# A dense expert mixer whose last 32 tokens take fetched rows instead, with the second table stationary and the gates multiplied on Pool

## The reference, cut to what matters

```python
def peer(xn, w_pq, sub_keys, expert_u, expert_v):       # 8 heads, 16 experts each, of 128*128
    ...
    idx = jnp.take_along_axis(cand_i, sel, axis=-1)
    gates = jax.nn.softmax(top_s, axis=-1)
    def block(args):
        x_blk, i_blk, g_blk = args
        pre = jnp.einsum('tkd,td->tk', expert_u[i_blk], x_blk)
        act = jax.nn.gelu(pre, approximate=False) * g_blk
        return jnp.einsum('tk,tkd->td', act, expert_v[i_blk])

h = h + peer(rms_norm(h, norm_ffn), ...)
gate = jax.nn.sigmoid(rms_norm(h, norm_ple) @ w_ple_gate)
h = h + gate * (p @ w_ple_proj)
return rms_norm(h, norm_final)
```

## Time and profile before

| | |
|---|---|
| time, median of 3 runs | 2223.78 us (2223.14 to 2226.92) |
| the profiled execution's own time | 2223.5 us |
| its span, first to last instruction | 2221.6 us |
| granted TensorE clock, mean | 0.985 of full speed |
| busy: PE, DVE, ACT, Pool | 97%, 69%, 48%, 26% of the span |

### The profile page before, as it was taken

One profiled execution on the slowest core, in us unless ns is written; L12 is line 12 of the kernel. 1 busy time (PEld: TensorE's weight loads), 2 busy tenths in 40 slices (PEclk: granted clock), 3 DMA queues, 4 the chain that ended last, 5 costly groups with the idle time before them and its releaser, 6 DMA issues.

```text
span 2221.6 us, 36663 instructions
## 1 busy us (share of the span) xinstructions
PE 2157.7 (97%) x11170; PEld 1847.3 (83%) x11170; DVE 1532.7 (69%) x2283; ACT 1074.0 (48%) x1444; POOL 573.7 (26%) x295
## 2 busy tenths in 40 slices
PE   7999999979999999999999999999999999999997
PEld 7888878978888888888888888888888888887886
DVE  6885777965547888888865555676677666666665
ACT  6543665234445444444444444545555454555454
POOL 0121000000000688888888881000000000000000
PEclk9999997999999999999999999999999999999998
DMA  5754559035544677777776665766666555654563
GB/s 193 257 184 159 189 178 352 1 128 194 182 170 167 183 182 187 187 184 188 183 195 189 189 188 187 241 244 245 243 241 239 195 190 195 234 191 170 195 202 141
DMA packets 157129, 431.01 MB, mean 194 GB/s; under 512 B 49552, under 2 KB 49936, under 8 KB 155408
## 3 DMA queue, kind: packets, MB, share of 16 engines
q1 hardware_dynamic: 118080, 417.59, 54.4%
q0 software_dynamic: 36864, 0.15, 4.0%
q10 hardware_dynamic: 2128, 12.58, 1.5%
HBM read 409.15 MB, written 21.10 MB: 194 GB/s over the span
## 4 chain that ended last, share of the span: by engine, by line
PE 89%; DVE 5%; DVEq 2%; issue 2%; ACT 1%; DMA 1%; ACTq 0%; SPq 0%
PE ps L237 25%; PE ps L1702 21%; PE ps L241 13%; PE ps L1709 10%; PE ps L262 5%; PE ps L256 5%; PE ps L257 5%; DVE lo L220 1%; PE ps L337 1%; ACT hi L214 1%; PE ps L1599 1%; PE ps L1555 1%; PE ps L1607 1%; DMA raw<-in_w_in_cols 0%; DVEq L879 0%
## 5 line engine op out<-in xcount | busy, mean ns | idle before, releaser
L220 DVE TENSOR_TENSOR lo<-raw,hi 128x1024 fp32r<-128x1024 f32 x724 | 892.6, 1237 | 427.0 <-ACT hi L214 402.4
L214 ACT ACTIVATE hi<-raw 128x1024 fp32r<-128x1024 f32 x724 | 762.7, 1055 | 634.0 <-PE ps L237 442.4
L237 PE MATMUL ps<-act_pair,hi 128*128 128x512 f32 x2816 | 707.8, 393 | 3.7 <-ACT hi L214 3.7
L1459 POOL DMA_INDIRECT gate_map<-gate_in_sb x256 | 529.6, 2069 | 439.9 <-DVEq L1299 361.2
L237 PEld LDWEIGHTS ps<-act_pair,hi 128*128 128x128 f32 x2816 | 507.3, 189 | 96.1 <-ACT hi L214 5.1
L241 PEld LDWEIGHTS ps<-act_pair,lo 128*128 128x128 f32 x2816 | 383.3, 190 | 34.0 <-DVE lo L220 7.3
L241 PE MATMUL ps<-act_pair,lo 128*128 128x256 f32 x2816 | 393.6, 283 | 3.9 <-DVE lo L220 3.9
L1702 PE MATMUL ps<-hi,stage_hi 128*128 128x512 f32 x1024 | 274.3, 390 | 3.3 <-DVE stage_lo L1320 3.2
L1709 PE MATMUL ps<-lo,stage_hi 128*128 128x512 f32 x1024 | 274.5, 390 | 0.0
L1702 PE MATMUL ps<-hi,stage_lo 128*128 128x512 f32 x1024 | 274.2, 390 | 0.0
L802 ACT ACTIVATE stage_hi<-arena 128x256 fp32r (+1 forms) x256 | 107.0, 418 | 344.8 <-PE ps L1709 340.1
(11 more groups left out here) (226 smaller groups left out, 1197.5 us busy)
## 6 DMA issues: line engine op xcount, KB each, us to landing
raw<-in_expert_u SPq DMA_DIRECT2D x256, 512.0 KB
raw<-in_expert_v SPq DMA_DIRECT2D x256, 512.0 KB
raw<-in_w_in_cols SPq DMA_DIRECT2D x64, 512.0 KB
raw<-in_w_in_rows SPq DMA_DIRECT2D x48, 512.0 KB
gate_map<-stage_lo SPq DMA_DIRECT2D x1, 16384.0 KB, 47.4
raw<-in_w_out SPq DMA_DIRECT2D x32, 512.0 KB
raw<-in_w_pq SPq DMA_DIRECT2D x32, 512.0 KB
gate_in_sb<-gate_map SPq DMA_DIRECT2D x32, 512.0 KB, 4.1
```

What stands on the lines that cost most here:

```text
L214: act.activation(hi[:, use, :], raw[:, slot, :], ACT.Copy).then_inc(hi_ready, 1)
L220: dve.tensor_tensor(lo[:, use, :], raw[:, slot, :], hi[:, use, :].bitcast(F32), ALU.subtract).then_inc(lo_ready, 1)
L237: mm = pe.matmul(out_ap, hi[:, use, d8 * P:(d8 + 1) * P], act_pair[:, d, :], start=(d == 0), stop=False)
L1459: pool.indirect_dma_start(gate_map, bass.IndirectOffsetOnAxis(ap=place[:, unit, r:r + 1], axis=0), gates_out[:, unit, r:r + 1], None, comp ...
```

## The change

**Tokens.** The two dense stages take the first 224 tokens (`MANY`). PE moves 448 columns where it moved 512 and 224 where it moved 256 in the U stage; `pre`, the activations, the map and its blocks (448 KB) shrink alike. The scatter of every second unit of gates takes 96 of 128 partitions.

**The V stage.** The table's 128x128 blocks are now held and the activations moved: 8 matmuls of 448 columns with `hi` and 8 of 224 with `lo` for each tile. Sums are channels by tokens and fill all eight banks in either half. Before half 1 may use a bank, DVE empties it (`take_half(0)`, 8 reductions, placed behind the first tile of half 1); behind the last tile comes `take_half(1)`, and `expert_rows` turns the sums back into rows with fp32 matmuls. The tiles are loaded straight out of the table as given: partition p of tile c reads 4 KB of row 128p + c, so neighbouring partitions read 1 MB apart, where before a tile was one contiguous 512 KB.

**The last 32 tokens.** Their 128 picks are dealt to four groups of 32 partitions, 32 steps for each. ACT writes picks, gates and scales to HBM and reads them back spread over the partitions (3 and 17 DMAs, in the last 96 tiles of the U stage). In the V stage Pool fetches for each of 64 steps (32 for the first table, 32 for the second) two halves of 128 x 4 KB by indirect DMA (`gather`), with one buffer for each half; a half is fetched when DVE has used the one before it. DVE's `few_half` multiplies and sums 1024 elements of each partition. Its places are fixed: behind tiles 2, 3, 5, 7 ... 125 of half 0 (64 places, 125/64 tiles apart, rounded down) for the first table, and behind tiles 136 to 248 of the 256 (114/64 apart) for the second. A matmul with a selector adds the four groups.

**The gates.** `apply_gates` moves from DVE to Pool (128x896 instead of 128x1024). Pool's order is `apply_gates(0)`, then for n = 0, 1, ... `apply_gates(n + 1)` (while n + 1 < 32) and `gather(n)`. SP loads block j of the map, as before, behind the table's block j-2 and only once `apply_gates(j-2)` is done.

**What follows.** The tiles of `w_ple` and the first transpose leave half 1 and come behind `expert_rows`, ahead of the gate stage; the second transpose now stands ahead of the first gate tile. DVE's order there is `rest_tile` for `w_ple` tile 0, `take_half(1)`, `add_experts(0)`, tile 1, `add_experts(1)`, tile 2, `take_ple(0)`, first `dve_turn`, tile 3, `take_ple(1)`, `dve_scale`, `take_ple(2)`, gate tile 0, `take_ple(3)`, second `dve_turn`.

The diff, cut to its core:

```diff
+FEW = 32
+MANY = SEQ - FEW
...
-T_PLE = T_V + CHUNKS + PLE_CHUNK
-T_GATE = T_V + 2 * CHUNKS + 4
+T_PLE = T_V + 2 * CHUNKS
+T_GATE = T_PLE + 4
...
-                mm = pe.matmul(out_ap, hi[:, use, d8 * P:(d8 + 1) * P], act_pair[:, d, :], start=(d == 0), stop=False)
+                mm = pe.matmul(first_tokens(out_ap), hi[:, use, d8 * P:(d8 + 1) * P], first_tokens(act_pair[:, d, :]),
+                               start=(d == 0), stop=False)
...
-                mm = pe.matmul(out_ap[:, 0:SEQ], lo[:, use, d8 * P:(d8 + 1) * P], act_hi[:, 8 * k + d8, :],
+                mm = pe.matmul(out_ap[:, 0:tokens], lo[:, use, d8 * P:(d8 + 1) * P], act_hi[:, 8 * k + d8, 0:tokens],
...
+            v_tiles = v_table.rearrange("(p c) (h f) -> h c p f", c=CHUNKS, h=2)
...
-                    load_tile(sp, n, slot, expert_v[ds(j * RAW + k, 1)].rearrange("a p f -> (a p) f"))
+                    n, slot, _, _ = tile_at(T_V + CHUNKS * half, j, RAW, k)
+                    load_tile(sp, n, slot, v_tiles[half][ds(j * RAW + k, 1)].rearrange("a p f -> (a p) f"))
...
+            for g in range(FEW_GROUPS):
+                at = slice(g * FEW, (g + 1) * FEW)
+                picks = slice(g * FEW_STEPS, (g + 1) * FEW_STEPS)
+                act.dma_start(few_index[at], few_ids.rearrange("s q h r -> s q (h r)")[:, :, picks]).then_inc(few_read, 16)
+                act.dma_start(few_gate[at], few_gates.rearrange("s h r -> s (h r)")[:, picks]).then_inc(few_read, 16)
+                act.dma_start(few_stat[at], few_scales).then_inc(few_read, 16)
+                act.dma_start(x_few[at], h_spill[MANY:SEQ, :]).then_inc(few_rows_in, 16)
+            act.dma_start(few_rows, norm_ffn.partition_broadcast(P)).then_inc(few_rows_in, 16)
...
-            def apply_gates(j, buf, turn):
-                dve.wait_ge(map_landed[buf], 16 * turn + 16)
-                a = experts[:, ds(G_CHUNKS * j, G_CHUNKS), :]
-                dve.tensor_tensor(a, a, gate_in_sb[:, buf].rearrange("p (c t) -> p c t", c=G_CHUNKS),
-                                  ALU.mult).then_inc(gated, 1)
-
-            apply_gates(0, 0, 0)
...
+            def few_half(n, q):
+                r, c = n % FEW_STEPS, slice(TILE * q, TILE * (q + 1))
+                dve.wait_ge(few_landed[q], 16 * n + 16)
+                if n < FEW_STEPS:
+                    e = dve.tensor_tensor_reduce(few_rows[:, c], few_rows[:, c], x_few[:, c], 1.0, 0.0, ALU.mult, ALU.add,
+                                                 few_part[:, 2 * r + q:2 * r + q + 1])
+                elif r == 0:
+                    e = dve.tensor_scalar(few_sum[:, c], few_rows[:, c], few_act[:, 0:1], None, ALU.mult)
+                else:
+                    e = dve.scalar_tensor_tensor(few_sum[:, c], few_rows[:, c], few_act[:, r:r + 1], few_sum[:, c],
+                                                 ALU.mult, ALU.add)
...
+            FEW_U_FROM, FEW_U_TO, FEW_V_FROM, FEW_V_TO = 2, 127, 136, 250
+            for k, (n, q) in enumerate(halves_u):
+                FEW_AT[FEW_U_FROM + k * (FEW_U_TO - FEW_U_FROM) // len(halves_u)] = lambda n=n, q=q: few_half(n, q)
...
+            for k, (n, q) in enumerate(halves_v):
+                FEW_AT[FEW_V_FROM + k * (FEW_V_TO - FEW_V_FROM) // len(halves_v)] = lambda n=n, q=q: few_half(n, q)
...
                 v = CHUNKS * half + 4 * i + c
                 dve.wait_ge(stage_hi_ready, v + 1)
-                dve.tensor_tensor(stage_lo[:, c % 2:c % 2 + 1, :], experts[:, ds(4 * i + c, 1), :],
-                                  stage_hi[:, c % 2:c % 2 + 1, :].bitcast(F32), ALU.subtract).then_inc(stage_lo_ready, 1)
-                rest_tile(dve, T_V + v + late, c % RAW, c % SPLIT)
-
-            def gated_block(j, buf, turn, first=False):
+                dve.tensor_tensor(stage[:, c % 2:c % 2 + 1, MANY:2 * MANY], experts[:, ds(4 * i + c, 1), :],
+                                  stage[:, c % 2:c % 2 + 1, 0:MANY].bitcast(F32), ALU.subtract).then_inc(stage_lo_ready, 1)
+                rest_tile(dve, T_V + v, c % RAW, c % SPLIT)
...
+            def take_half(half):
+                dve.wait_ge(lo_used, T_V + CHUNKS * (half + 1))
+                for b in range(8):
+                    dve.tensor_reduce(v_cols[half][:, b], ps[:, b, 0:2 * MANY].rearrange("p (h t) -> p t h", h=2), AX_X,
+                                      ALU.add).then_inc(v_taken, 1)
...
+            for i in range(CHUNKS // 4):
                 for c in range(4):
                     value_tile(1, i, c)
+                    if i == 0 and c == 0:
+                        take_half(0)
+                    few_work(1, i, c)
...
+                        n = P if unit % TB == 0 else FEW_FROM
...
+            def apply_gates(j):
+                pool.wait_ge(map_landed[j % 2], 16 * (j // 2) + 16)
+                if j == G_BLOCKS - 1:
+                    pool.wait_ge(expert_bank, CHUNKS + 2)
+                a = experts[:, ds(G_CHUNKS * j, G_CHUNKS), :]
+                pool.tensor_tensor(a, a, gate_in_sb[:, j % 2, 0:G_CHUNKS * MANY].rearrange("p (c t) -> p c t", c=G_CHUNKS),
+                                   ALU.mult).then_inc(gated, 1)
+
+            def gather(n):
+                r, table = n % FEW_STEPS, u_table if n < FEW_STEPS else v_table
+                for q in range(2):
+                    if n >= 1:
+                        pool.wait_ge(few_done, 2 * n + q - 1)
+                    pool.indirect_dma_start(few_rows[:, q * TILE:(q + 1) * TILE], None,
+                                            table.rearrange("e (h f) -> (e h) f", h=2),
+                                            bass.IndirectOffsetOnAxis(ap=few_index[:, q, r:r + 1], axis=0)
+                                            ).then_inc(few_landed[q], 16)
+
+            pool.wait_ge(expert_bank, CHUNKS - 2)
+            apply_gates(0)
+            pool.wait_ge(few_read, 16 * 3 * FEW_GROUPS)
+            pool.wait_ge(x_few_ready, 2)
+            for n in range(2 * FEW_STEPS):
+                if n + 1 < G_BLOCKS:
+                    apply_gates(n + 1)
+                gather(n)
 
...
-                    for k, a in enumerate((stage_hi, stage_lo)):
-                        for tb in range(TB):
-                            for b in range(2):
-                                mm = pe.matmul(ps[:, 4 * half + 2 * tb + b, :], a[:, use, tb * P:(tb + 1) * P],
-                                               hi[:, use, b * 512:(b + 1) * 512], start=(first and c == 0 and k == 0),
-                                               stop=False, skip_group_check=True)
+                    for b in range(8):
+                        if first and c == 0 and half == 1:
+                            pe.wait_ge(v_taken, b + 1)
+                        if first and c == 0 and half == 0 and b >= U_BANK:
+                            pe.wait_ge(pre_ready, CHUNKS - 1 + b - U_BANK)
+                        mm = pe.matmul(ps[:, b, 0:2 * MANY], hi[:, use, b * P:(b + 1) * P], stage[:, use, 0:2 * MANY],
+                                       start=(first and c == 0), stop=False, skip_group_check=True)
                     mm.then_inc(hi_used, 1)
-                    pe.wait_ge(lo_ready, T_V + v + late + 1)
-                    for tb in range(TB):
-                        for b in range(2):
-                            mm = pe.matmul(ps[:, 4 * half + 2 * tb + b, :], stage_hi[:, use, tb * P:(tb + 1) * P],
-                                           lo[:, use, b * 512:(b + 1) * 512], start=False, stop=False,
-                                           skip_group_check=True)
+                    pe.wait_ge(lo_ready, T_V + v + 1)
+                    for b in range(8):
+                        mm = pe.matmul(ps[:, b, 0:MANY], lo[:, use, b * P:(b + 1) * P], stage[:, use, 0:MANY],
+                                       start=False, stop=False, skip_group_check=True)
...
+            def expert_rows(half):
+                pe.wait_ge(v_taken, 8 + (4 if half == 0 else 8))
+                for tb in range(TB):
+                    if tb == 1:
+                        pe.wait_ge(selector_few_ready, 1)
+                        pe.wait_ge(few_done, 4 * FEW_STEPS)
+                        for q in range(2):
+                            c = slice(TILE * half + 512 * q, TILE * half + 512 * (q + 1))
+                            pe.matmul(ps[:, 4 * half + 2 + q, :], selector_few, few_sum[:, c], start=True, stop=False,
+                                      skip_group_check=True)
+                    n = P if tb == 0 else FEW_FROM
+                    for b in range(8):
+                        mm = pe.matmul(ps[0:n, 4 * half + 2 * tb + b // 4, (b % 4) * P:(b % 4 + 1) * P],
+                                       v_cols[half][:, b, tb * P:tb * P + n], ident, start=(tb == 0), stop=True,
+                                       skip_group_check=True)
+                    mm.then_inc(rows_done, 1)
+
...
+            for half in range(2):
+                value_round(half, 0, first=True)
```

(33 more changed lines are left out.)

293 lines of the change are left out of this document (181 added, 112 removed).

## The result

The changed kernel takes 2294.4 us (median of 4 runs, 2289.9 to 2299.0) where the kernel before takes 2224.1: 1.0314 times as long, interval 1.0302 to 1.0327. The forecast was 2206 us, range 2155 to 2265. It is slower, by more than the range allowed.

A forecast was written before the change was run, and what follows sets the result against it. The prediction took PE, busy 97% of the span, as the bound, with DVE close behind in U. Its terms, -26 - 15 + 4 + 32 + 4 - 28 + 11 = -18 us, gave 2206 us, range 2155 to 2265.

The forecast's parts named there:

- PE's tiles: PE's matmuls in both stages: a tile takes 2.51 us in U and 2.50 in V, 224 columns costing 0.112.
- U stage, plain tiles: The 96 U tiles without the choice: 26 us less, DVE's work hidden.
- U stage with the choice: The 160 U tiles with the choice: 15 us less, bounds 8 and 26, with some DVE waiting left.
- ACT's 17 issues: ACT's DMA issues in the U stage: some 8 us on ACT, of which 4 reach PE (0 to 6).
- Half 0: V's first half: 380 us, 32 more than before, bounds 341 and 418, at 2.8 us a tile plus 21 of waits.
- the shortfall is shared by the two stalls that lie within each distance: Half 0's waits for fetched rows: shortfalls of 0.8 and 3.6 us a block, shared, make 21 us.
- Pool's multiply: Half 0: `apply_gates` on Pool still costs DVE 2.1 us, more than the 1.14 it saves.
- Between the halves: PE's first tile of half 1 waits bank by bank for `take_half(0)`: 4 us (3 to 6).
- Half 1: V's second half: DVE at 2.1 us a tile under PE's 2.50, so 28 us less (bounds 20 and 33).
- The tail: From V's end to the gate stage: 32 us (28 to 36), net 11 us more (5 to 18).
- The fetch loop is longer: Rival on V: at a 17.5 us loop half 0 takes 418 us, half 1 loses 6, total 2250; chance 0.19.
- The table's tiles land more slowly: Rival on V: 1 MB pitch slows tile loads, half 0 some 25 us longer, half 1 8, total 2239; chance 0.08.

The follow-up runs named there:

- two_buffers_early: The changed kernel with a second pair of buffers for fetched halves, and gathers ahead of the multiply by the next block's gates: 2203.3 us.
- gates_on_dve: The changed kernel with the multiply by the gates moved from Pool back to DVE, single buffers: 2232.0 us.
- no_rows: The changed kernel without gathers and with only two of 128 few_half operations, so the last 32 tokens' experts are left out: 2174.1 us.
- Two buffers alone: The changed kernel with a second pair of buffers for fetched halves, Pool's order unchanged: 2255.9 us.
- best: The changed kernel with gates on DVE, a second buffer pair, ACT's 17 DMA issues spread over nine rounds, and a contiguous copy of the second table: 2168.5 us.
- v_contiguous: The changed kernel with the second table's tiles loaded from a copy in which each tile is one contiguous 512 KB: 2259.8 us.
- before_raw_table: The kernel before the change with its second table's tiles read from the table as given, partitions 1 MB apart: 2225.2 us against 2224.3.

## Why the prediction was wrong, point by point

- **PE's tiles**: right. 2.51 us measured against 2.51 and 2.50; 224 columns cost 0.11.
- **U stage, plain tiles**: right. 5.05 us a chunk, 48 x (5.59 - 5.05) = 25.9 against 26 (the forecast's own product, 96 x 0.28, is 27).
- **U stage with the choice**: 10.5 us of the 15 forecast (chunks 0 to 79 take 440.7 us against 451.2), within the bounds of 8 and 26. A row was misread here: the rest tile at 682.33 is U tile 1's, since PE's first U tile begins at 674.71, so the 448.6 us are 159 tiles of 2.82. The sum, which went by the 56.5 us of 20 tiles, is not touched by it.
- **ACT's 17 issues**: 7.4 us instead of 4. ACT is held 8.9 us in one piece, near the 8 of the forecast (ACT's timeline: the first issue, and the rounding behind the last); ACT's lead swallowed less of it than I took it to, and went beyond the upper end of 6.

```profile
1217.68 0.62 ACTq L837 DMA_DIRECT2D few_index<-few_ids  x1
...
1227.60 2.00 ACT L223 ACTIVATE hi<-raw 128x1024 fp32r<-128x1024 f32 x2 [8.91 <-issue]
```

- **Half 0**: 411 instead of 380, beyond the forecast's size but inside its bounds (341 to 418). The mechanism was the named one, and `two_buffers_early` and `gates_on_dve` show it. The loop from the map's issue was forecast at 14.8 us, and where DVE waited it takes 13.8 to 19.0, median 15.4: near as a sum, but with other parts that made up for one another (medians: 7.5 until Pool's multiply instead of 5.1 and 1.1, multiply 2.5, fetch with descriptors 5.8 instead of 6.5). The term that failed is the next one, "the shortfall is shared by the two stalls that lie within each distance", and with it that blocks 1 to 11 have no shortfall: 21 us were put down for waits. Without fetches half 0 takes 350.4 us, so the fetches and the waits for them cost 61. In the first 44 tiles, where I had none, a tile took 3.1 us too: there the fetches that DVE waited for landed 7 to 8.6 us behind their issue, not 4.1 + 2.4, and the loop was 17.5 us and more where six tiles of 2.8 us give 16.8.
- **Pool's multiply**: right. It holds DVE for 1.94 of its 2.12 us.
- **Between the halves**: half 1's first 16 tiles are 5 us longer than their neighbours in `no_rows`; 4 forecast.
- **Half 1**: the step that failed, 52 of the 92 us by which the span missed (375.6 against 320 + 4; half 0 missed by 32, the U stage by 7, the tail by 1). The forecast said "a half has 3.6 tiles, 8.9 us, from its buffer's release to its use, and needs 2.4 + 4.1". The fetch took 8.9 us itself, descriptors in it, since the landing was taken from a map block in the traffic of before. And 3.6 tiles lie from use to use, so DVE's own 1.3 us belong in the loop. 10.2 us were needed where 8.9 were there. Then I checked DVE's and PE's sums for this half (2.1 under 2.50) and read from that that nothing else could bind. Two buffers alone give 327.3. What the 8.9 us are made of, beyond the pitch's half microsecond in half 1, was not measured apart.
- **The clock**: no term of the forecast. Of PE's 787 us in V (1371.85 to 2159.1), 256 undisturbed tiles are 643 and its waits 97; about 47 remain. The lower level can account for at most 31 of them (half of its 61 us); in its 16 stretches the matmuls take some 28 us longer. Most of the other 20 lie in single steps at or near a wait, some 0.16 us before it and 0.10 behind it; what causes them is open. In `best` the clock is 1.00 through half 0 and falls once, between the halves.
- **The tail**: right. The gate's first tile starts 33.4 us after V's last product (forecast 32; timeline of PE, against the earlier trace rows), 12.3 us net against 11.

```profile
2158.24 1.05 PE L1835 MATMUL ps<-stage,lo 128*128 128x224 f32 x8
...
2192.49 0.48 PE L269 MATMUL ps<-hi,act_pair 128*128 128x512 f32 x1
```

Of the rivals, two were right at once. *The fetch loop is longer* gave 418 us for half 0, but only 6 us for half 1; it should have been worked out for half 1 with the same care. *The table's tiles land more slowly* gave 33 us where `v_contiguous` shows 35, and I gave it 0.08; that the sizes agree is luck in part, for it had the engines full in half 0 (0.99), and they are 0.83 busy. They are no alternatives: the second is part of why the first holds. The range counted them one at a time, and so ended at 2265.

Behind the row of `before_raw_table` stands the rule of the Trainium skill (DMA: Bandwidth & Descriptors, Latency and other measured facts) that rates fall where HBM rows lie a large power of two apart; by that rule, the trace agrees, at 1 MB: 48.3 MB took 74.6% of the engines instead of 67.6%. The same page's fit for Pool's queue (Anatomy of one DMA, SWDGE path), 3.2 us for 512 KB by my estimate, is not what these traces show under load: 4.2 us at the least, 8.9 in half 1.

## What to carry to other kernels

For each transfer that is waited for, write down its loop from release to next use, with the user's own time in it and the landing as it is under the load of the changed kernel, and divide by the distance in tiles; sums of busy time per tile say nothing on that. Don't put a prefetch behind an operation that itself waits for another transfer on an in-order queue: in half 0 turning two lines round was worth 50 us, with two buffers in place, and the second buffer without it nothing. Give rivals that feed one another a chance together, not one at a time.
